# Stick-breaking attention: the scores of two units in one run with both masks behind them, running sums grouped by matrix over both heads

## The chip, the cores and the metric

The kernel runs on one core of one Trainium2 chip. The metric is device time in microseconds; the time before is the median of 3 runs. A profile of one execution gives busy times, waits and the order of instructions.

## The reference

The whole program is two transformer blocks over 512 positions of 1024 features, in float32. The first has an MLP, a mixer of windowed attention and gated linear attention, and a second MLP. The second is a stack of two layers; each has a mixer, a cross-attention into 256 memory tokens and a gated MLP with a short convolution. The mixer of the last layer is the one that is changed here: strictly causal stick-breaking attention, 16 heads of 64 features.

```
z = (q . k) * scale                      # per head, 512 x 512
log_beta = log_sigmoid(z)
log_1m   = where(strict, log_sigmoid(-z), 0)
tail     = reverse cumsum(log_1m) - log_1m
a        = where(strict, exp(log_beta + tail), 0)
out      = a @ v
```

In the kernel's terms this is a = exp(z - (softplus(z) of this key and of all later keys up to the query)), with masked places at -1e30 before the exponential.

## The kernel before

**Work of a pair.** Heads are taken in pairs (t = 0 to 7; j = 0, 1 in a pair), since two heads of 64 features fill 128 partitions. The scores lie transposed in PSUM: 128 keys of a block kb down the partitions, the queries kb*128 to 511 along the columns. The four key blocks are dealt to three *units*: unit 0 holds blocks 3 and 2 (128 + 256 columns per head), unit 1 block 1 (384), unit 2 block 0 (512). A unit has two PSUM banks, one per head, which serve for z and then, with the sums added onto them, for the exponent.

**Steps of a unit.**
1. TensorE, `stick_scores(t, u)`: keys times queries in float32 with 64 rows of contraction (L1267; each is recorded as two matmuls, and the two heads use different halves of the array), then one matmul per head with an identity that adds the mask onto the diagonal block (L1272). The last one raises `z_done`. For t > 0 the function first waits for `a_made` of the pair before, that is until ScalarE has read the unit's banks.
2. ScalarE, `soft`: exponential (L1862) and logarithm of 1 + it (L1864), which is softplus.
3. VectorE, `softplus`: a clamp that reads z from PSUM (L2766), then the split of the value in a rounded part `hi` (L2768) and a rest `lo` (L2770). That raises `softplus_cut`.
4. TensorE, `stick_exponent(t, u)`: after waiting for `softplus_cut` it adds the negated sums onto z. L1282 multiplies the unit's own hi and lo by matrix 0 of `od_later` (minus a triangle of ones: sums within the key block), L1291 multiplies the parts of later key blocks by matrix 1 (minus all ones). It raises `arg_ready`.
5. ScalarE, `weights`: exponential into `od_a` (L1868), which raises `a_made`.
6. TensorE, `stick_out(t)`: `od_a` times the values (L1303, 16 matmuls), once all three units of the pair are there; VectorE copies the result out (L2775).

**Order.** Each engine runs its own queue in program order. TensorE's order for a pair is: scores of unit 1, scores of unit 2, `stick_out` of the pair before, exponents of units 0 and 1, scores of unit 0 of the next pair, exponent of unit 2. ScalarE's is soft 1, soft 2, weights 0, weights 1, soft 0 of the next pair, weights 2. VectorE's is softplus 1, softplus 2, copy of the pair before, softplus 0 of the next pair. Ahead of the loop stand the scores of units 0 and 1 of pair 0 and one slab of the value projection (L623 to L625); ScalarE's `soft(0, 1)` is behind a wait for the end of that slab. Behind the loop stands the output projection (L605 to L607), as everywhere else in the program a stream of 512-column matmuls over weight slabs.

Of the kernel before, what the change touches and what calls it, by code (L numbers as in the profile page):

```python
# [15 lines left out]
P = 128  # L16
SEQ = 512
# [8 lines left out]
NB = SEQ // P  # L26
# [36 lines left out]
UNITS = [(3, 2), (1,), (0,)]  # L63
UNIT_COLUMNS = [FAR, 3 * P, 4 * P]
# [36 lines left out]
def block_at(kb):  # L101

    return [2, 1, 0, 0][kb], P if kb == 2 else 0
# [49 lines left out]
def build(nc, wstream, gains, conv_w, lam_in, base, rope, later, gla_masks, alibi, gate_up,  # L153
          x_in, p_in, mem_in, out):
    ctx = ExitStack()
    with ctx:
        def sb(name, shape, dt=FP32, scope=ctx):
            return scope.enter_context(nc.sbuf_tensor(name, shape, dt))

        def sem(name):  # L160
            return ctx.enter_context(nc.semaphore(name))
# [46 lines left out]
        with ExitStack() as s:  # L208
            od_q = sb("od_q", [P, KT, SEQ], FP32, s)
            od_k = sb("od_k", [P, KT, SEQ], FP32, s)  # L210
# [24 lines left out]
        ident_r = sb("ident_r", [P, P], FP32R)  # L235
# [51 lines left out]
        with ExitStack() as s:  # L287
            od_v = sb("od_v", [P, NB, D], FP32, s)
            od_mask = sb("od_mask", [P, 3, P], FP32, s)
            od_later = sb("od_later", [P, 3, P], FP32R, s)  # L290
            od_a = sb("od_a", [P, 2, TRI], FP32, s)
        ps = ctx.enter_context(nc.psum_tensor("ps", [P, 8, SEQ], FP32))
# [93 lines left out]
        z_done = sem("z_done")  # L386
# [4 lines left out]
        a_made = sem("a_made")  # L391
# [14 lines left out]
        def pair_of(c):  # L406

            if AT_MIX1 + MIX1_FIRST <= c < AT_MIX1 + MIX1_FIRST + 2:
                return 0
            if AT_MIX1 + MIX1_SLABS <= c < AT_MIX1 + MIX1_SLABS + DOWN:  # L410
                return [5, 0, 2, 5][c - AT_MIX1 - MIX1_SLABS]
            if AT_EVEN + EVEN_FIRST <= c < AT_EVEN + EVEN_SLABS:
                return 2
            if c == AT_EVEN + EVEN_SLABS:
                return 6
            return 2 * (c % 2)
# [27 lines left out]
        def gl_turned(t, n):  # L444

            return gl_k[:, t, n]
# [33 lines left out]
        def k_to_end():  # L480

            return m1_c[:, 0:2 * SEQ].rearrange("p (t n) -> p t n", t=2)
# [16 lines left out]
        def unit_bank(u):  # L499

            return [4, 6, pair_of(AT_ODD + ODD_SLABS - 2)][u]
# [9 lines left out]
        def unit_parts(t, u):  # L511

            at, w = UNIT_AT[u], UNIT_COLUMNS[u]
            if u == 0 and t % 2 == 0:
                tiles = (od_s_even, od_hi_even, od_lo_even)
            else:
                tiles = (od_s, od_hi, od_lo)
            return [tile[:, :, at:at + w] for tile in tiles]
# [5 lines left out]
        def spread(ap, n):  # L524

            return ap.unsqueeze(1).to_broadcast([ap.shape[0], n, ap.shape[1]])
# [53 lines left out]
        def _(pe):  # L580
            n = {"cut": 0, "cuts": 0, "op": 0, "h": 0, "sq": 0, "job": 0, "it": 0, "xsq": 0, "norm": 0, "pair": 0}
            mm_ = nc.tensor.matmul
# [31 lines left out]
            def to_positions(c, cols=256, beside={}):  # L614

                start_slab(c)
                wh = w_hi[:, c % 4, :].rearrange("p (k n) -> p k n", k=KT)
                wl = w_lo[:, c % 4, :].rearrange("p (k n) -> p k n", k=KT)
                for r in range(NB):
                    o = acc_rows(c)[:, r, 0:cols]  # L620
                    for k in range(KT):
                        xh, xl = op_hi[:, k, r * P:(r + 1) * P], op_lo[:, k, r * P:(r + 1) * P]
                        mm_(o, xh, wh[:, k, 0:cols], start=(k == 0), stop=False)  # L623
                        mm_(o, xl, wh[:, k, 0:cols], start=False, stop=False)  # L624
                        mm = mm_(o, xh, wl[:, k, 0:cols], start=False, stop=(k == KT - 1))  # L625
                    if r == NB - 1:
                        mm.then_inc(slab_done, 1)
                    if r in beside:
                        beside[r]()
# [307 lines left out]
            for t in range(2):  # L937
                for b in range(NB - 1):
                    mm = nc.tensor.transpose(ps[:, 4 + t, b * P:(b + 1) * P], k_to_end()[:, t, b * P:(b + 1) * P], ident)
# [3 lines left out]
            for b in range(NB - 1):  # L943
                for t in range(2):
                    for j in range(2):
                        h = 2 * t + j
                        mm = mm_(ps[64 * j:64 * j + 64, 6 + t, b * P:(b + 1) * P],
                                 gl_turned(t, slice(b * P + 64 * j, b * P + 64 * j + 64)),
                                 m1_gv[:, b, h * P:(h + 1) * P],
                                 start=True, stop=True)  # L950
# [7 lines left out]
            for b in range(1, NB):  # L958
                for t in range(2):
                    for j in range(2):  # L960
# [3 lines left out]
                            skip_group_check=True)  # L964
            for bp in range(2):
                pe.wait_ge(gl_c_ready, 2 * (LEVELS - MASKED) + bp + 1)
                for j in range(2):
                    for b in range(2):
                        for t in range(2):
                            h, blk = 2 * t + j, 2 * bp + b  # L970
                            mm = mm_(ps[:, h, blk * P:(blk + 1) * P], m1_gv[:, blk, h * P:(h + 1) * P],
                                     gl_a[:, bp, 4 * j + 2 * b + t, :], start=False, stop=(blk == NB - 1),
                                     skip_group_check=True)
# [282 lines left out]
            for d in range(8, 11):  # L1256
                to_positions(AT_ODD + d)

            def stick_scores(t, u):


                if t:
                    pe.wait_ge(a_made, 3 * (t - 1) + u + 1)
                for kb in UNITS[u]:
                    b, at = unit_bank(u), block_at(kb)[1]
                    for j in range(2):
                        mm_(ps[:, b + j, at:at + SEQ - kb * P], od_k[64 * j:64 * j + 64, t, kb * P:(kb + 1) * P],  # L1267
                            od_q[64 * j:64 * j + 64, t, kb * P:SEQ], start=(kb == UNITS[u][0]), stop=False,
                            skip_group_check=True)
                w = len(UNITS[u]) * P  # L1270
                for j in range(2):
                    mm = mm_(ps[:, b + j, 0:w], ident_r[:], spread(od_later[:, 2, :], len(UNITS[u])), start=False,  # L1272
                             stop=True, skip_group_check=True)
                mm.then_inc(z_done, 1)

            def stick_exponent(t, u):

                pe.wait_ge(softplus_cut, 3 * t + u + 1)
                for j in range(2):
                    _, hi, lo = unit_parts(t, u)  # L1280
                    for part in (hi, lo):
                        mm_(ps[:, unit_bank(u) + j, 0:UNIT_COLUMNS[u]], od_later[:, 0, :], part[:, j, :],  # L1282
                            start=False, stop=True, skip_group_check=True)
                    for kb in UNITS[u]:
                        z = block_at(kb)[1]
                        for b in range(kb + 1, NB):
                            (of, at), w = block_at(b), SEQ - b * P
                            a0 = z + (b - kb) * P
                            _, hi, lo = unit_parts(t, of)
                            for part in (hi, lo):  # L1290
                                mm = mm_(ps[:, unit_bank(u) + j, a0:a0 + w], od_later[:, 1, :],  # L1291
                                         part[:, j, at:at + w], start=False, stop=True, skip_group_check=True)
                mm.then_inc(arg_ready, 1)

            def stick_out(t):
                if t >= 2:
                    pe.wait_ge(o_read, t - 1)
                for kb in reversed(range(NB)):
                    (of, at), w = block_at(kb), SEQ - kb * P
                    pe.wait_ge(a_made, 3 * t + of + 1)  # L1300
                    at += UNIT_AT[of]
                    for j in range(2):
                        mm = mm_(ps[64 * j:64 * j + 64, stick_bank(t), kb * P:SEQ],  # L1303
                                 od_v[:, kb, (2 * t + j) * 64:(2 * t + j + 1) * 64], od_a[:, j, at:at + w],
                                 start=(kb == NB - 1), stop=(kb == 0), skip_group_check=True)
                mm.then_inc(stick_ready, 1)

            pe.wait_ge(later_ready, 1)
            stick_scores(0, 0)
            stick_scores(0, 1)  # L1310
            to_positions(AT_ODD + ODD_SLABS - 1)
            n["op"] += KT
            pe.wait_ge(acc_free, AT_ODD + ODD_SLABS + 1)
            for t in range(PAIRS):
                if t:
                    stick_scores(t, 1)
                stick_scores(t, 2)
                if t == 1:
                    pe.wait_ge(acc_free, AT_ODD + ODD_SLABS + 2)
                if t:  # L1320
                    stick_out(t - 1)
                stick_exponent(t, 0)
                stick_exponent(t, 1)
                if t < PAIRS - 1:
                    stick_scores(t + 1, 0)
                stick_exponent(t, 2)
            stick_out(PAIRS - 1)
            project(AT_ODD + ODD_SLABS)
# [6 lines left out]
        def _(act):  # L1335
# [522 lines left out]
            def soft(t, u):  # L1858

                buf, _, _ = unit_parts(t, u)  # L1860
                act.wait_ge(z_done, 3 * t + u + 1)
                f_(buf, unit_z(u), ACT.Exp).then_inc(a_step, 1)  # L1862
                done(a_step)
                f_(buf, buf, ACT.Ln, bias=1.0).then_inc(sp_ready, 1)  # L1864
# [1106 lines left out]
```

## Time and profile before

| | |
|---|---|
| median of 3 runs | 2562.7 us (2562.1 to 2562.7) |
| span of the profiled execution | 2561.3 us |
| PE busy | 2541.6 us, 99% |
| DVE (VectorE) busy | 1596.4 us, 62% |
| ACT (ScalarE) busy | 912.6 us, 36% |
| stick-breaking stretch | about 1875 to 1984 us of the span |

The profiled execution's time is known here by its span; the median of the runs is 1.4 us above it. PE is TensorE's matmuls, PEld its weight loads. Matmuls are pipelined: start times are exact, ends are modelled, so the distance from one start to the next says more than a duration. A matmul row such as `64*128 64x384` has 64 rows of contraction and 384 columns.

### The profile page before, as it was taken

The page shows a single profiled execution, that of the slowest core. Times are in us where ns is not written, and L with a number is a line of the kernel's source. Part 1 is how long each engine was busy: PE and PEld are TensorE (multiplying, and loading weights), DVE is VectorE, ACT ScalarE, POOL GpSimd, SP SyncE. Part 2 cuts the span into 40 slices and gives each one's busy share as a digit, 9 for nine tenths or more (in the row PEclk, how much of TensorE's full clock was granted, in tenths as well). Part 3 has the DMA queues.
Part 4 walks back from the last instruction along what each step waited for, and adds up shares of the span by engine and source line. Part 5 has one row for each costly group of instructions (what it writes and reads, how often), then busy time and mean ns, then how long its engine had stood idle before and what let it go on. Part 6 is the DMA issues. An engine that isn't in the chain of part 4 may idle for free.

```text
span 2561.3 us, 31974 instructions
## 1 busy us (share of the span) xinstructions
PE 2541.6 (99%) x12548; PEld 2107.0 (82%) x12548; DVE 1596.4 (62%) x1976; ACT 912.6 (36%) x1184; POOL 10.2 (0%) x24
## 2 busy tenths in 40 slices
PE   8999999999999999999999999999999999999999
PEld 7888888778888888877898888888886888888887
DVE  6444468866444468677765747476357665775755
ACT  5222234543222245344443423233146343432322
POOL 0000001000000000000000000000000000000000
PEclk9999999999999999999999999999999999999999
DMA  5222233112222232212321232323210232232222
GB/s 182 102 83 99 96 110 120 67 50 96 103 89 98 99 115 101 99 50 99 132 94 63 104 103 82 115 83 123 94 66 13 87 116 83 84 115 83 101 96 82
DMA packets 37410, 241.91 MB, mean 94 GB/s; under 512 B 4416, under 2 KB 7280, under 8 KB 9136
## 3 DMA queue, kind: packets, MB, share of 16 engines
q1 hardware_dynamic: 34736, 233.78, 26.3%
q10 hardware_dynamic: 1920, 5.22, 0.6%
q0 software_dynamic: 640, 1.31, 0.2%
q8 instruction: 81, 1.33, 0.2%
q14 instruction: 33, 0.27, 0.0%
HBM read 236.89 MB, written 2.10 MB: 93 GB/s over the span
## 4 chain that ended last, share of the span: by engine, by line
PE 93%; DVE 5%; ACT 1%; issue 1%; DMA 0%; POOL 0%; DVEq 0%; ACTq 0%
PE ps L605 24%; PE ps L607 24%; PE ps L606 24%; PE ps L1234 1%; PE ps L623 1%; PE ps L625 1%; PE ps L624 1%; PE ps L766 1%; PE ps L1267 1%; PE ps L1291 1%; PE ps L1282 1%; DVE w_lo L2048 1%; PE ps L768 1%; PE ps L767 1%; PE ps L1303 1%
## 5 line engine op out<-in xcount | busy, mean ns | idle before, releaser
L605 PE MATMUL ps<-op_hi,w_hi 128*128 128x512 f32 x2056 | 800.9, 390 | 0.2 <-DVE op_lo L1929 0.2
L606 PE MATMUL ps<-op_lo,w_hi 128*128 128x512 f32 x2056 | 800.5, 389 | 0.0
L607 PE MATMUL ps<-op_hi,w_lo 128*128 128x512 f32 x2056 | 800.4, 389 | 0.0
L1350 ACT ACTIVATE w_hi<-w_raw 128x2048 fp32r<-128x2048 f32 x217 | 414.4, 1911 | 485.2 <-PE ps L607 315.3
L2048 DVE TENSOR_TENSOR w_lo<-w_raw,w_hi 128x2048 fp32r<-128x2048 f32 x217 | 497.0, 2292 | 38.7 <-ACT w_hi L1350 22.3
L605 PEld LDWEIGHTS ps<-op_hi,w_hi 128*128 128x128 f32 x2056 | 386.3, 188 | 81.4 <-issue 1.4
L607 PEld LDWEIGHTS ps<-op_hi,w_lo 128*128 128x128 f32 x2056 | 386.2, 188 | 80.6
L606 PEld LDWEIGHTS ps<-op_lo,w_hi 128*128 128x128 f32 x2056 | 386.3, 188 | 80.3
L2013 DVE SCALAR_TENSOR_TENSOR x<-ps,x 128x512 f32<-128x512 f32 x134 | 92.7, 691 | 310.8 <-PE ps L607 293.0
L605 PE MATMUL ps<-h_hi,w_hi 128*128 128x512 f32 x692 | 269.5, 389 | 0.0
L606 PE MATMUL ps<-h_lo,w_hi 128*128 128x512 f32 x692 | 269.2, 389 | 0.0
L607 PE MATMUL ps<-h_hi,w_lo 128*128 128x512 f32 x692 | 269.2, 389 | 0.0
L2096 DVE TENSOR_TENSOR sil<-ps,rs_x 128x512 f32<-128x512 f32 x44 | 30.4, 692 | 212.2 <-PE ps L607 209.1
L1463 ACT ACTIVATE conv_buf<-u_buf,cw 128x512 f32<-128x512 f32 x88 | 63.2, 726 | 260.9 <-DVE u_buf L2079 260.9
L605 PEld LDWEIGHTS ps<-h_hi,w_hi 128*128 128x128 f32 x692 | 129.9, 188 | 27.6 <-DVE h_lo L2107 0.6
L606 PEld LDWEIGHTS ps<-h_lo,w_hi 128*128 128x128 f32 x692 | 129.9, 188 | 27.0
L607 PEld LDWEIGHTS ps<-h_hi,w_lo 128*128 128x128 f32 x692 | 129.9, 188 | 26.9
L1468 ACT ACTIVATE sil<-sil 128x512 f32<-128x512 f32 x44 | 27.9, 634 | 338.2 <-DVE sil L2096 338.1
L2079 DVE TENSOR_TENSOR u_buf<-ps,rs_x 128x512 f32<-128x512 f32 x44 | 30.4, 692 | 82.1 <-PE ps L607 82.1
L2088 DVE SCALAR_TENSOR_TENSOR conv_buf<-u_buf,cw,conv_buf 128x511 f32<-128x511 f32 x88 | 66.1, 751 | 20.5 <-ACT conv_buf L1463 11.0
L1395 ACT ACTIVATE sq<-x 128x512 f32<-128x512 f32 x80 | 48.3, 623 | 77.8 <-DVE sums L1941 74.1
L2091 DVE SCALAR_TENSOR_TENSOR conv_buf<-u_buf,cw,conv_buf 128x510 f32<-128x510 f32 x88 | 66.0, 750 | 10.5 <-DVE conv_buf L2088 1.4
(373 smaller groups left out, 3085.7 us busy)
## 6 DMA issues: line engine op xcount, KB each, us to landing
w_raw<-in_wstream_dram SPq DMA_DIRECT2D x217, 1024.0 KB, 4.8
cr_m<-in_mem_dram ACTq DMA_DIRECT2D x2, 1024.0 KB, 4.9
w_raw<-in_wstream_dram SPq DMA_DIRECT2D x7, 256.0 KB, 8.0
x<-in_x_dram SPq DMA_DIRECT2D x3, 512.0 KB, 7.3
out_dram<-x SPq DMA_DIRECT2D x3, 512.0 KB, 2.6
m_s<-m_q POOLq DMA_DIRECT2D x16, 64.0 KB, 2.5
ev_s<-in_alibi_dram ACTq DMA_DIRECT2D x1, 1024.0 KB, 4.9
m_c<-in_rope_dram ACTq DMA_DIRECT2D x1, 640.0 KB, 3.9
```

The costliest lines, as they stand in the source:

```text
L605: mm_(o, w_hi[:, c % 4, w], hi[:, k, 0:cols], start=(k == 0), stop=False)
L606: mm_(o, w_hi[:, c % 4, w], lo[:, k, 0:cols], start=False, stop=False)
L607: mm = mm_(o, w_lo[:, c % 4, w], hi[:, k, 0:cols], start=False, stop=(k == kt - 1))
L1350: f_(w_hi[:, c % 4, :], w_raw[:, c % 2, :], ACT.Copy).then_inc(w_hi_ready, 1)
L1395: f_(to[:, n["xsq"] % 2, 0:src.shape[1]], src, ACT.Square).then_inc(xsq_ready, 1)
L1463: f_(conv_buf[:, j, :], u_buf[:, j, :], ACT.Copy, scale=tap).then_inc(tap_ready, 1)
L2013: ins = v.scalar_tensor_tensor(x[:, 2 * d + j, :], acc(c, j), half, x[:, 2 * d + j, :], ALU.mult, ALU.add)
L2048: v.tensor_tensor(w_lo[:, c % 4, :], w_raw[:, c % 2, :], w_hi[:, c % 4, :].bitcast(FP32), ALU.subtract).then_inc(w_ready, 1)
L2079: v.tensor_tensor(u_buf[:, 0, :], acc(c, 0), rs_x[:], ALU.mult).then_inc(scaled_ready, 1)
L2088: v.scalar_tensor_tensor(buf[:, 1:SEQ], u[:, 0:SEQ - 1], w1, buf[:, 1:SEQ], ALU.mult, ALU.add).then_inc(v_step, 1)
L2091: v.scalar_tensor_tensor(buf[:, 2:SEQ], u[:, 0:SEQ - 2], w0, buf[:, 2:SEQ], ALU.mult, ALU.add).then_inc(v_step if j else conv_ready, 1)
L2096: v.tensor_tensor(sil[:, c % 2, :], acc(c, 0), rs_x[:], ALU.mult).then_inc(scaled_ready, 1)
```

## The change

`stick_scores` takes a list of units: it issues the scores of all of them and then the masks of all of them, raising `z_done` after each unit's mask. The wait for `a_made` of each unit stands before that unit's scores, and so ahead of both masks. Units 1 and 2 of a pair (and units 0 and 1 of pair 0) are issued that way. In `stick_exponent` the loops over heads and matrices are exchanged: units 0 and 2 issue all matmuls with matrix 0 for both heads and then all with matrix 1; unit 1 the other way round. Number and sizes of matmuls are the same. ScalarE's and VectorE's programs are not touched.

```diff
-            def stick_scores(t, u):
-                if t:
-                    pe.wait_ge(a_made, 3 * (t - 1) + u + 1)
-                for kb in UNITS[u]:
-                    b, at = unit_bank(u), block_at(kb)[1]
+            def stick_scores(t, units):
+                for u in units:
+                    if t:
+                        pe.wait_ge(a_made, 3 * (t - 1) + u + 1)
+                    for kb in UNITS[u]:
+                        b, at = unit_bank(u), block_at(kb)[1]
+                        for j in range(2):
+                            mm_(ps[:, b + j, at:at + SEQ - kb * P], od_k[64 * j:64 * j + 64, t, kb * P:(kb + 1) * P],
+                                od_q[64 * j:64 * j + 64, t, kb * P:SEQ], start=(kb == UNITS[u][0]), stop=False,
+                                skip_group_check=True)
+                for u in units:
+                    w = len(UNITS[u]) * P
                     for j in range(2):
-                        mm_(ps[:, b + j, at:at + SEQ - kb * P], od_k[64 * j:64 * j + 64, t, kb * P:(kb + 1) * P],
-                            od_q[64 * j:64 * j + 64, t, kb * P:SEQ], start=(kb == UNITS[u][0]), stop=False,
-                            skip_group_check=True)
-                w = len(UNITS[u]) * P
+                        mm = mm_(ps[:, unit_bank(u) + j, 0:w], ident_r[:], spread(od_later[:, 2, :], len(UNITS[u])),
+                                 start=False, stop=True, skip_group_check=True)
+                    mm.then_inc(z_done, 1)
+
+            def sums_within(t, u):
+                _, hi, lo = unit_parts(t, u)
                 for j in range(2):
-                    mm = mm_(ps[:, b + j, 0:w], ident_r[:], spread(od_later[:, 2, :], len(UNITS[u])), start=False,
-                             stop=True, skip_group_check=True)
-                mm.then_inc(z_done, 1)
+                    for part in (hi, lo):
+                        mm = mm_(ps[:, unit_bank(u) + j, 0:UNIT_COLUMNS[u]], od_later[:, 0, :], part[:, j, :],
+                                 start=False, stop=True, skip_group_check=True)
+                return mm
+
+            def sums_of_later(t, u):
+                pairs = [(kb, b) for kb in UNITS[u] for b in range(NB - 1, kb, -1)]
+                for kb, b in pairs:
+                    (of, at), w = block_at(b), SEQ - b * P
+                    a0 = block_at(kb)[1] + (b - kb) * P
+                    _, hi, lo = unit_parts(t, of)
+                    for j in range(2):
+                        for part in (hi, lo):
+                            mm = mm_(ps[:, unit_bank(u) + j, a0:a0 + w], od_later[:, 1, :], part[:, j, at:at + w],
+                                     start=False, stop=True, skip_group_check=True)
+                return mm
 
             def stick_exponent(t, u):
                 pe.wait_ge(softplus_cut, 3 * t + u + 1)
-                for j in range(2):
-                    _, hi, lo = unit_parts(t, u)
-                    for part in (hi, lo):
-                        mm_(ps[:, unit_bank(u) + j, 0:UNIT_COLUMNS[u]], od_later[:, 0, :], part[:, j, :],
-                            start=False, stop=True, skip_group_check=True)
-                    for kb in UNITS[u]:
-                        z = block_at(kb)[1]
-                        for b in range(kb + 1, NB):
-                            (of, at), w = block_at(b), SEQ - b * P
-                            a0 = z + (b - kb) * P
-                            _, hi, lo = unit_parts(t, of)
-                            for part in (hi, lo):
-                                mm = mm_(ps[:, unit_bank(u) + j, a0:a0 + w], od_later[:, 1, :],
-                                         part[:, j, at:at + w], start=False, stop=True, skip_group_check=True)
+                if u == 1:
+                    sums_of_later(t, u)
+                    mm = sums_within(t, u)
+                else:
+                    sums_within(t, u)
+                    mm = sums_of_later(t, u)
                 mm.then_inc(arg_ready, 1)
@@
-            stick_scores(0, 0)
-            stick_scores(0, 1)
+            stick_scores(0, [0, 1])
             to_positions(AT_ODD + ODD_SLABS - 1)
@@
             for t in range(PAIRS):
-                if t:
-                    stick_scores(t, 1)
-                stick_scores(t, 2)
+                stick_scores(t, [1, 2] if t else [2])
@@
                 if t < PAIRS - 1:
-                    stick_scores(t + 1, 0)
+                    stick_scores(t + 1, [0])
                 stick_exponent(t, 2)
```

## Rows read from the trace of the kernel before

**Rows 1.** The page: span, and busy time of TensorE with its instructions.

```profile
span 2561.3 us, 31974 instructions
...
PE 2541.6 (99%) x12548; PEld 2107.0 (82%) x12548; DVE 1596.4 (62%) x1976; ACT 912.6 (36%) x1184; POOL 10.2 (0%) x24
```

**Rows 2.** Timeline: start us, us, instruction; scores of units 1 and 2, pair 2.

```profile
1911.39 0.27 PE L1291 MATMUL ps<-od_lo,od_later 128*128 128x128 f32 x1
1911.59 0.92 PE L1267 MATMUL ps<-od_q,od_k 64*128 64x384 f32 x4
1911.70 1.02 ACT L1868 ACTIVATE od_a<-ps 128x1024 f32<-128x1024 f32 x1 [0.81 <-PE ps L1291]
1912.43 0.44 PE L1272 MATMUL ps<-od_later,ident_r 128*128 128x128 f32 x2
1912.81 1.13 PE L1267 MATMUL ps<-od_q,od_k 64*128 64x512 f32 x4
1912.91 0.81 ACT L1862 ACTIVATE od_s<-ps 128x768 f32<-128x768 f32 x1 [0.19 <-PE ps L1272]
1913.86 0.44 PE L1272 MATMUL ps<-od_later,ident_r 128*128 128x128 f32 x2
...
1914.23 2.37 PE L1303 MATMUL ps<-od_a,od_v 128*64 128x128 f32 x16
```

**Rows 3.** Timeline of the same pair, from VectorE's split of unit 1 on.

```profile
1916.29 0.96 DVE L2770 TENSOR_TENSOR od_lo<-od_s,od_hi 128x768 fp32r<-128x768 f32 x1
...
1917.74 0.39 PE L1282 MATMUL ps<-od_hi,od_later 128*128 128x384 f32 x1
...
1919.27 1.23 DVE L2770 TENSOR_TENSOR od_lo<-od_s,od_hi 128x1024 fp32r<-128x1024 f32 x1
...
1920.55 0.19 PEld L1282 LDWEIGHTS ps<-od_hi,od_later 128*128 128x128 f32 x1
...
1923.23 0.92 PE L1267 MATMUL ps<-od_q,od_k 64*128 64x384 f32 x4
```

**Rows 4.** Timeline of the last pair, t = 7.

```profile
1971.13 0.81 ACT L1862 ACTIVATE od_s<-ps 128x768 f32<-128x768 f32 x1 [0.19 <-PE ps L1272]
...
1977.48 1.23 DVE L2770 TENSOR_TENSOR od_lo<-od_s,od_hi 128x1024 fp32r<-128x1024 f32 x1
...
1978.76 0.19 PEld L1282 LDWEIGHTS ps<-od_hi,od_later 128*128 128x128 f32 x1 [1.17 <-DVE od_lo L2770]
...
1979.10 0.39 PE L1282 MATMUL ps<-od_lo,od_later 128*128 128x512 f32 x1
...
1979.98 0.27 PE L1291 MATMUL ps<-od_lo,od_later 128*128 128x128 f32 x1
...
1980.09 0.45 PE L1282 MATMUL ps<-od_hi,od_later 128*128 128x512 f32 x1
...
1980.38 0.39 PE L1282 MATMUL ps<-od_lo,od_later 128*128 128x512 f32 x1
...
1980.61 0.34 PE L1291 MATMUL ps<-od_hi,od_later 128*128 128x384 f32 x1
...
1981.46 2.37 PE L1303 MATMUL ps<-od_a,od_v 128*64 128x128 f32 x16
```

**Rows 5.** Waits, 1888 to 1984 us: who <- whom: us in total, times, longest.

```profile
ACT od_s L1862 <- PE ps L625: 10.5, 1, 10.5
...
PEld ps L1282 <- DVE od_lo L2770: 3.5, 3, 2.0
```

**Rows 6.** Timeline: scores and mask of unit 0 ahead of the loop.

```profile
1876.30 0.50 PE L1272 MATMUL ps<-od_later,ident_r 128*128 128x256 f32 x2
...
1876.74 0.92 PE L1267 MATMUL ps<-od_q,od_k 64*128 64x384 f32 x4
```

**Rows 7.** Busy time by stretch: length, engines (instructions), granted clock PEclk, DMA.

```profile
1888.00:1900.00 12.00, 10.03 (x68) 8.14 (x66) 7.84 (x9) 6.80 (x8) 0.00 (x0) 1.00 0.00 0
```

## The prediction

> **What bounds the kernel now.** I read the page first, then the stretch of the trace where the changed lines run, then its instructions in order of time. The page gives PE 2541.6 us busy in a span of 2561.3 us [rows 1]. Read alone, that says that a shorter TensorE program is a shorter kernel. But matmul ends are modelled, so a PE that has just been released can still look busy. The question is what releases it inside the stick-breaking stretch, from about 1875 to 1984 us.
>
> Take one pair t of the loop, from the start S of `stick_scores(t, 1)` at 1911.59 to the next one at 1923.23: 11.64 us [rows 2, 3]. Follow it from S. The scores of unit 1 and its mask raise `z_done`, and ScalarE starts its exponential at 1912.91, 1.32 us after S [rows 2]. The two activations and then VectorE's six instructions for units 1 and 2 follow. The last one starts at 1919.27 and ends 1.23 us later, at 1920.50 [rows 3]. PE loads the weights of `stick_exponent(t, 2)` at 1920.55, 0.05 us after that end. From there to the next S are 2.68 us. So 1.32 + 7.64 + 2.68 = 11.64 us: the whole period is one loop through PE, ScalarE and VectorE.
>
> Is this loop the bound, or does it only keep step with a PE that is full? The last pair answers. There no scores stand between `stick_exponent(7, 1)` and `stick_exponent(7, 2)`, and PE visibly waits, 1.17 us, for `od_lo`. From the start of unit 1's exponential (1971.13) to that release (1978.76) are 7.63 us, the lag of VectorE's end (1977.48 + 1.23 = 1978.71) to the weight load is again 0.05 us, and from the load to the instruction after the exponent matmuls (1981.46) are 2.70 us [rows 4]. The undisturbed pair has the same three numbers. Hence its slack is about zero: what delays `z_done` of unit 1 lengthens every pair by the same amount, and PE time saved ahead of `stick_exponent(t, 2)` buys nothing. The view of waits hides this: it books only 3 such waits on VectorE, 3.5 us in all [rows 5].
>
> **The change part by part.** No matmul is added or removed; 8 pairs run.
>
> *Where PE waits for the previous weights.* `stick_scores(t, 2)` waits for `a_made` of (t-1, 2), ScalarE's exponential over 1024 columns. It started at 1911.70, 0.11 us after S, took 1.02 us, and the scores of unit 2 started at 1912.81, 0.09 us after its end [rows 2]. Before, unit 1's mask ran in this time, and `z_done` of unit 1 was out before the wait. After, that mask stands behind the wait and behind the scores of unit 2. This is the largest term.
>
> *Delay of `z_done` of unit 1.* After the change the exponential starts about 0.06 us behind S (see the running sums), takes 1.02, and the release takes 0.09: scores of unit 2 start at S + 1.17. From their start to a mask matmul are 1.05 us (1912.81 to 1913.86), and from the mask's start to ScalarE's exponential 0.48 us (1912.43 to 1912.91) [rows 2]. Sum: 1.17 + 1.05 + 0.48 = 2.70 us where it was 1.32: +1.38. Bounds: without the wait for `a_made` only the scores of unit 2 would stand in between, 512 columns in the four passes that the rows show (128 more columns cost 1912.81 to 1913.86 less 1911.59 to 1912.43 = 0.21 us, so 512 cost 0.85): +0.85. If restarting after the wait costs what it costs the exponent matmuls, 0.34 from first to second instead of 0.23 [rows 4]: +1.49. I take +1.38, the wait being in the code and its end in the rows.
>
> *Fewer switches among scores and masks.* Going from a 64-row score matmul to the mask and back has a price: the mask of unit 1 holds PE from 1912.43 to 1912.81, 0.38 us, where its 256 columns stream in 0.11 (at one pass, 512 take 0.21). That is 0.27 too much, and a group of scores has a fill of its own: 1911.59 to 1912.43 is 0.84 us for 384 columns in four passes, 0.64, so 0.20 [rows 2]. The Trainium skill, "TensorEngine Tiling (Array Packing)", Key Properties, says that a change of tiling mode drains the engine. The trace agrees (0.38 us for 0.11); by that rule alone the change would save one round of it per pair, about 0.45 us, and some 3.6 us in all. In the loop the room that this frees is filled by the wait for `a_made`, so for t >= 1 I take zero. Once, before the loop, it is real: `stick_scores(0, [0, 1])` stands behind TensorE's own projection. There the mask of unit 0 took 1876.30 to 1876.74, 0.44 us for 0.21 of streaming [rows 6], plus the second fill of 0.20: -0.43 us. It counts because ScalarE's `soft(0, 1)` waits 10.5 us for the end of the following projection [rows 5].
>
> *Running sums by matrix.* Before, `stick_exponent(t, 2)` goes from 128-column sums of the second matrix back to 512-column ones of the first between the heads. The steps are 0.11 (1979.98 to 1980.09) and 0.29 (to 1980.38), then 0.23 (to 1980.61) [rows 4]. With 0.055 (a quarter of the streaming of 512) and 0.23 as the regular steps for 128 and 512 columns, the return costs 0.11 us. After the change I add starts: 0.34 + 3 x 0.23 for the four 512-column ones, 4 x 0.055, 4 x 0.115, 4 x 0.17 for later sums of 128, 256, 384, and 0.145 for the switch to scores (1911.39 to 1911.59 less 0.055 [rows 2]). That is 2.54 us for 2.68: -0.14. Bounds: 0 (another such return appears where widths grow from 128 to 256) and -0.29 (every overhead but one restart and one switch gone: 5120 columns in 2.13 us, + 0.11 + 0.145). The last matmul is now 384 wide and ends 0.34 + 0.03 us after its start, while S comes 0.16 + 0.145 after it: the exponential starts 0.06 us after S, used above. The same grouping in units 0 and 1 saves about 0.11 us each, on PE time that waits anyway: zero. If that cover were gone it would be 0.22 x 8 = 1.8 us gained.
>
> *Is something else late next?* `stick_exponent(t, 1)` waits for VectorE's unit 1: 1916.29 + 0.96 is 4.34 us after ScalarE's start [rows 3], so 2.70 + 4.34 + 0.05 = 7.09 us after S. From its start to the load of `stick_exponent(t, 2)` it took 1917.74 to 1920.55, 2.81 us with `stick_scores(t + 1, 0)` in it; with 0.11 for the restart that ends at 10.01. VectorE releases at 2.70 + 7.64 = 10.34. So PE waits twice per pair, VectorE stays the releaser, with 0.33 us to spare. Behind the waiting PE stand `stick_out(t - 1)` (2.37 us, [rows 2]) and `stick_exponent(t, 0)`; their customers, ScalarE's weights 0 and VectorE's copy, have over 1 us of room.
>
> *Sum.* Period after: 2.70 + 7.64 + 2.54 = 12.88 us, +1.24. Seven pairs carry it (t = 1 to 7): +8.7. Pair 0 has unit 1 long done and only gets the shorter exponent: -0.14. Start: -0.43. Total +8.1 us, span 2569.4. Behind the stretch PE streams weights as before, so it is passed on whole. The span shown is 1.4 us under the median; added to the median of 2562.7, the time is 2570.8 us.
>
> **The rivals.**
> 1. *The loop has slack, PE is the bound.* Then the added delay is absorbed, and the grouping pays: 8 x 0.36 + 0.43 = -3.3 us, 2559.4, not slower. It decides only if the slack per pair is over 1.2 us; for it speaks PE's 99% [rows 1], against it the equal 0.05 us and 2.7 us in a pair that waits and in one that seems not to [rows 3, 4]. Slack s under that takes off 7s. Chance 5%.
> 2. *`a_made` holds nothing back.* Scores 2 follow scores 1 directly, +0.85 instead of +1.38: 7 x (0.85 - 0.14) - 0.57 = +4.4 us, 2567.1, within the resolution. For it: the scores of unit 2 may have started at 1912.81 because the mask took that long. Against: the exponential ended at 1912.72, and it can't start before the last exponent matmul [rows 2]. With a large gain from grouping this is also the low edge. Chance 9%.
> 3. *Two restarts make PE late again.* If restarts cost over 0.33 us more than counted in `stick_exponent(t, 1)`, or the wait for `a_made` costs a restart of its own, each 0.1 us is 0.7 us: +9 to +12, 2572 to 2575. Chance 11%.
> 4. *The clock falls.* PE now stands for about 1 us and twice 0.3 us per pair. In 1888 to 1900 us, with waits for VectorE of that size, the granted clock was 1.00, the 2.4 GHz level [rows 7]. At the 1.2 GHz level the roughly 9 us of streaming in a pair (a period of 11.64 less waits and fills) would double: 7 x 9 = some +60 us, 2630. The Trainium skill, "TensorE: Matmul & The Clock Gate", in "Why this matters for your kernels", warns of idle gaps between bursts of matmuls; no row here shows a fall. Chance 1%.
>
> **How the numbers follow.** The forecast has 74%; its own range, from +1.38 (-0.06, +0.11) and -0.14 (+0.14, -0.15) times 7, less 0.57, is +6.6 to +9.9: 2569.3 to 2572.6. The 80% range adds part of rivals 2 and 3: 2567.5 to 2573.5. A measurement of this kernel tells about 0.2%, 5.1 us, from no change. Slower by more: forecast, 3 and 4, 86%, less 1 for a mixture with rival 2: 85%. Within: rival 2, most of rival 1: 13%. Faster by more: 2%, rival 1 with rival 2.
>
> **What the profile after would show.** Right: period from S to S near 12.9 us; ScalarE's exponential of unit 1 starting 2.6 to 2.8 us after S; the first score matmul of unit 2 within 0.1 us of the end of ScalarE's weights; the view of waits full of PE on `od_lo`, seven or more at unit 1 (about 1 us) and at unit 2 (about 0.3 us); 7.6 us from that exponential to the load of `stick_exponent(t, 2)`; 2.5 us from there to S; the projection before the loop 0.4 us earlier. Wrong: a period under 11.6 us (rival 1); scores of unit 2 in one run with unit 1 (rival 2); PE reaching `stick_exponent(t, 2)` behind VectorE (rival 3); a granted clock under 1 (rival 4).

## The result, and the profile after

The changed kernel takes 2572.4 us (median of 5 runs, 2571.38 to 2575.3) against 2562.7 us (5 runs, 2561.55 to 2562.85): 9.7 us more. The ratio of the runs is 1.0041, 95% interval 1.0029 to 1.0054: slower (the quotient of the two medians is 1.0038). The forecast was 2570.8 us, with a range of 2567.5 to 2573.5.

The page of the kernel after, its span and its busy time by engine:

```profile
span 2570.6 us, 31974 instructions
...
PE 2543.8 (99%) x12548; PEld 2105.2 (82%) x12548; DVE 1596.4 (62%) x1976; ACT 912.0 (35%) x1184; POOL 10.2 (0%) x24
```

Beside [rows 1] nothing seems to have happened: the same instructions, the same 99% on PE, 2 us more of it, and a span 9.3 us longer. Busy shares of the whole run don't tell this story. Over the stick-breaking stretch alone PE's share does fall, from 93.0 of 96 us (1888 to 1984) to 95.2 of 105 us (1888 to 1993), but only the order in time says why. The timeline of the kernel after, the same pair as in [rows 2, 3] (start us, us, engine, line, operation). L1267 are still the scores; the masks are now L1273, the sums within a block L1282, the later ones L1295, ScalarE's activations L1874, L1876 and L1880, VectorE's split L2782:

```profile
1912.14 0.92 PE L1267 MATMUL ps<-od_q,od_k 64*128 64x384 f32 x4
1912.25 1.02 ACT L1880 ACTIVATE od_a<-ps 128x1024 f32<-128x1024 f32 x1 [1.22 <-PE ps L1295]
...
1913.33 1.13 PE L1267 MATMUL ps<-od_q,od_k 64*128 64x512 f32 x4 [0.27 <-ACT od_a L1880]
...
1914.39 0.66 PE L1273 MATMUL ps<-od_later,ident_r 128*128 128x128 f32 x4
1914.86 0.81 ACT L1874 ACTIVATE od_s<-ps 128x768 f32<-128x768 f32 x1 [1.59 <-PE ps L1273]
...
1918.24 0.96 DVE L2782 TENSOR_TENSOR od_lo<-od_s,od_hi 128x768 fp32r<-128x768 f32 x1
...
1919.25 0.19 PEld L1295 LDWEIGHTS ps<-od_hi_even,od_later 128*128 128x128 f32 x1 [0.75 <-DVE od_lo L2782]
...
1921.21 1.23 DVE L2782 TENSOR_TENSOR od_lo<-od_s,od_hi 128x1024 fp32r<-128x1024 f32 x1
...
1922.49 0.19 PEld L1282 LDWEIGHTS ps<-od_hi,od_later 128*128 128x128 f32 x1 [0.28 <-DVE od_lo L2782]
...
1925.24 0.92 PE L1267 MATMUL ps<-od_q,od_k 64*128 64x384 f32 x4
```

The reader is to see four things. The period from S to S is 25.24 - 12.14 = 13.10 us; it was 11.64. ScalarE's weights of the pair before end at 13.27, and the scores of unit 2 follow at 13.33, with PE released by them. Unit 1's exponential starts 2.72 us after S; it was 1.32. And from there to the weight load of unit 2's exponent are 22.49 - 14.86 = 7.63 us, what they were. PE's weight loads now stand waiting for VectorE's split twice in the pair, for 0.75 and 0.28 us, where the same pair before shows no such wait.

The view of waits of the kernel after, over the stretch (who <- whom: us in total, times, longest):

```profile
PEld ps L1295 <- DVE od_lo L2782: 7.2, 8, 2.0
...
PEld ps L1267 <- ACT od_a L1880: 6.2, 7, 0.9
...
PEld ps L1282 <- DVE od_lo L2782: 3.6, 8, 1.7
```

Seven of the eight pairs wait for ScalarE's weights (`od_a`). All eight wait for VectorE at unit 1 (L1295) and at unit 2 (L1282); [rows 5] had three waits for VectorE in all.

Where the span's 9.3 us lie: seven pairs at 1.45 each are 10.15 us more, pair 0 about 0.05 more; 0.4 less from the run of units 0 and 1 ahead of the loop; and 0.5 less that was there before any changed instruction ran (the first score matmul starts at 1874.91, before at 1875.45), which belongs to the execution and not to the change.

### The profile page after: what moved, and what is told of

Its sections match the earlier page's. It is cut to its first block, busy times and chain, and to the rows that moved or that the text cites. A ratio compares the mean times of both kernels' runs of the same rounds, so it can differ in the third digit from the quotient of the medians.

```text
span 2570.6 us, 31974 instructions
## 1 busy us (share of the span) xinstructions
PE 2543.8 (99%) x12548; PEld 2105.2 (82%) x12548; DVE 1596.4 (62%) x1976; ACT 912.0 (35%) x1184; POOL 10.2 (0%) x24
## 4 chain that ended last, share of the span: by engine, by line
PE 90%; DVE 6%; ACT 2%; issue 1%; DMA 0%; DVEq 0%; ACTq 0%
PE ps L605 24%; PE ps L606 24%; PE ps L607 24%; PE ps L1234 1%; PE ps L623 1%; PE ps L625 1%; PE ps L624 1%; PE ps L766 1%; DVE w_lo L2060 1%; PE ps L768 1%; PE ps L767 1%; DVE od_lo L2782 1%; DVE od_s L2778 1%; PE ps L816 1%; PE ps L1195 1%
```

## The experiments

Each kernel was timed 5 to 11 times beside the kernel before on the same chip; differences are of medians, while a ratio with its 95% interval comes from all the runs and is not the quotient of the medians. The first four kernels shared a chip (before: 2562.24 us there), and so did the last three (2562.11 us).

**1. The run of scores alone.** `stick_scores` and its calls from the change, `stick_exponent` from before.

```diff
 # stick_scores(t, units), stick_scores(0, [0, 1]), stick_scores(t, [1, 2] if t else [2]): as in the change
-                if u == 1:
-                    sums_of_later(t, u)
-                    mm = sums_within(t, u)
...
+                for j in range(2):
+                    for part in (hi, lo):
+                        ...                        # L1282, then L1291, head by head
```

> Half of the change alone: units 1 and 2 (0 and 1 ahead of the loop) in one run with both masks behind it; exponent matmuls in the order of the kernel before. Zero slack in the loop through PE, ScalarE and VectorE: the wait for a_made ahead of both masks delays unit 1's exponential from 1.32 to about 2.75 us after S; period 11.64 + 1.4 = 13.05 us, 7 pairs +10, start -0.4: +9 to +10 us, as much as the whole change. Rival (PE is the bound): the run saves a switch per pair, -0.4 us in the loop, time same or a little less than before.

2571.16 us, +8.9; ratio 1.0038 (1.0024 to 1.0052). Its timeline (here ScalarE's exponential is L1860, its weights L1866):

```profile
1911.07 0.92 PE L1267 MATMUL ps<-od_q,od_k 64*128 64x384 f32 x4
...
1912.26 1.13 PE L1267 MATMUL ps<-od_q,od_k 64*128 64x512 f32 x4 [0.27 <-ACT od_a L1866]
...
1913.79 0.81 ACT L1860 ACTIVATE od_s<-ps 128x768 f32<-128x768 f32 x1 [1.59 <-PE ps L1273]
...
1924.11 0.92 PE L1267 MATMUL ps<-od_q,od_k 64*128 64x384 f32 x4
```

Period 13.04 us, the exponential 2.72 us after S, as expected; the time is just short of the +9 to +10 us. This half is nearly the whole of the loss.

**2. The grouped sums alone.** The change's `stick_exponent`, `sums_within` and `sums_of_later`; scores and masks as before.

```diff
 # stick_scores(t, u) and its calls: as before
+                if u == 1:
+                    sums_of_later(t, u)
+                    mm = sums_within(t, u)
+                else:
+                    sums_within(t, u)
+                    mm = sums_of_later(t, u)
```

> The other half alone: scores and masks as before, exponent matmuls grouped by matrix over both heads. If going back to the first matrix costs 0.11 us, as the prediction had it, the exponent of unit 2 shortens to 2.54 us and the time falls by 8 x 0.14 = 1.1 us. If the cost belongs to 128-column matmuls in a row (each asks for a weight load of its own, 0.11 us apart), four in a row cost what two pairs of them did: exponent of unit 2 2.7 to 2.75 us, period 11.64 to 11.75, time +0 to +0.6 us.

2562.9 us, +0.7; ratio 1.0004 (0.9995 to 1.0013). By time alone this decides little, by the trace more (sums within a block L1281):

```profile
1910.96 0.92 PE L1267 MATMUL ps<-od_q,od_k 64*128 64x384 f32 x4
...
1919.94 0.19 PEld L1281 LDWEIGHTS ps<-od_hi,od_later 128*128 128x128 f32 x1
...
1922.69 0.92 PE L1267 MATMUL ps<-od_q,od_k 64*128 64x384 f32 x4
```

The period is 11.73 us, and from the load of the exponent of unit 2 to S are 2.75 us, the figures of the second expectation. The grouping saves nothing there; it costs 0.07 us. The return to the first matrix, which the prediction priced, isn't what costs.

**3. VectorE's rounding of unit 1 twice.** Kernel before, 0.6 us more in the chain and nothing on PE.

```diff
-                v.tensor_copy(hi, buf).then_inc(v_step, 1)
-                done(v_step)
+                for _ in range(2 if u == 1 else 1):
+                    v.tensor_copy(hi, buf).then_inc(v_step, 1)
+                    done(v_step)
```

> The kernel before with VectorE's rounding of unit 1 done twice in every pair: 0.56 us of VectorE work and its 0.04 us of waiting in the chain, nothing on PE. Zero slack: period 11.64 + 0.6 = 12.24 us, 8 pairs: +4.8 us. PE is the bound and the chain has slack (rival 1 of the prediction, over 1.2 us): period 11.64, no change.

2567.06 us, +4.8; ratio 1.0020 (1.0011 to 1.0029). Its timeline:

```profile
1911.93 0.92 PE L1267 MATMUL ps<-od_q,od_k 64*128 64x384 f32 x4
...
1916.03 1.16 DVE L2769 CAST od_hi<-od_s 128x768 fp32r<-128x768 f32 x2
...
1921.48 0.19 PEld L1282 LDWEIGHTS ps<-od_hi,od_later 128*128 128x128 f32 x1 [0.31 <-DVE od_lo L2771]
...
1924.16 0.92 PE L1267 MATMUL ps<-od_q,od_k 64*128 64x384 f32 x4
```

In the kernel before the rounding of unit 1 is one instruction:

```profile
1915.69 0.56 DVE L2768 CAST od_hi<-od_s 128x768 fp32r<-128x768 f32 x1
```

Two take 1.16 us, 0.60 more, and the period is 12.23 us, 0.59 more. An engine that is busy 62% of the span was given 0.6 us more per pair, and all of it came out at the end: the chain has no slack that the trace can tell, although PE's row says 99%.

**4. Exponent matmuls ordered by width.** Kernel before; a 128-column matmul never follows another while a wider one is left, so the matrix alternates.

```diff
+                wide = [...]        # (bank, first column, width, matrix, moving part) of all matmuls of the unit
+                short = [m for m in wide if m[2] == P]
+                rest = [m for m in wide if m[2] > P]
+                order = []
+                for m in rest:
+                    order.append(m)
+                    if short:
+                        order.append(short.pop(0))
+                order += short
```

> Scores and masks as before; exponent matmuls ordered so that a 128-column one never follows another where a wider one is left, which changes the matrix at almost every matmul. If changing the matrix costs: exponent of unit 2 gets longer, by up to 0.1 us a change, time up. If 128-column matmuls in a row cost (weight loads 0.11 us apart against 0.055 us of streaming): the exponent of unit 2 falls from 2.68 to about 2.5 us, period about 11.45 to 11.5, time -1.2 to -1.5 us.

2562.89 us, +0.6; ratio 1.0004 (0.9995 to 1.0013). Both expectations missed. Nothing is gained: from the load of the exponent of unit 2 (1919.70) to S (1922.48) are 2.78 us, where 2.5 were expected. And the many changes of matrix don't cost up to 0.1 us each either. The steps tell what does cost; they follow below, under the third point.

**5. The wait for `a_made` alone, earlier.** Kernel before, no work moved.

```diff
                 w = len(UNITS[u]) * P
+                if t and u == 1:
+                    pe.wait_ge(a_made, 3 * (t - 1) + 3)
                 for j in range(2):
                     mm = mm_(ps[:, b + j, 0:w], ident_r[:], ...
```

> The kernel before with one wait moved: PE waits for a_made of the pair before (unit 2) already ahead of unit 1's mask, so scores 1, wait, mask 1, scores 2, mask 2. No work and no order of matmuls changes. Zero slack and the wait open at about S + 1.22: mask 1 at 1.22 instead of 0.84, unit 1's exponential at S + 1.70 instead of 1.32, period 12.02 us, 7 pairs: +2.7 us. Rival (the wait was open in any case when PE came to it): no change.

2564.47 us, +2.4; ratio 1.0009 (1.0000 to 1.0018), a difference at the edge of what the runs can tell, so the trace has to carry it. Its timeline (mask L1274, ScalarE's weights L1870, exponential L1864):

```profile
1922.66 0.92 PE L1267 MATMUL ps<-od_q,od_k 64*128 64x384 f32 x4
1922.77 1.02 ACT L1870 ACTIVATE od_a<-ps 128x1024 f32<-128x1024 f32 x1 [0.80 <-PE ps L1293]
...
1923.85 0.44 PE L1274 MATMUL ps<-od_later,ident_r 128*128 128x128 f32 x2 [0.27 <-ACT od_a L1870]
...
1924.32 0.81 ACT L1864 ACTIVATE od_s<-ps 128x768 f32<-128x768 f32 x1 [0.53 <-PE ps L1274]
...
1934.64 0.92 PE L1267 MATMUL ps<-od_q,od_k 64*128 64x384 f32 x4
```

The mask starts 0.06 us after the weights end, the exponential 1.66 us after S, and the period is 11.98 us, in every pair. The shift of the exponential and the growth of the period are both 0.34 us: one line that issues no work costs what it shifts `z_done` by.

**6. Unit 1's scores before the exponent of unit 2.** Unit 1 got buffers of its own for odd pairs, in free memory, so that ScalarE doesn't overwrite parts that PE still reads, and ScalarE's order was changed to match.

```diff
 # in the loop of TensorE, pair t
-                if t:
-                    stick_scores(t, 1)
                 stick_scores(t, 2)
...
                 if t < PAIRS - 1:
                     stick_scores(t + 1, 0)
+                    stick_scores(t + 1, 1)
                 stick_exponent(t, 2)
 # not shown: the buffers, and ScalarE's order (soft(t + 1, 1) ahead of weights(t, 2))
```

> The kernel before with unit 1's scores of the next pair moved ahead of the exponent of unit 2 (own buffers for unit 1 in odd pairs, ScalarE's order changed to match). VectorE's chain for unit 1 now starts some 4 us earlier, so it can't be late. What stays is PE's own wait for the weights of unit 2 with nothing in front of it: exponent of unit 2 to scores of unit 2 3.9 us from start to start, and the other steps of a pair 9.0 us: period about 12.9 us, +9 us. If only VectorE's chain counted and the wait were harmless: period 11.64 or less, time same or lower.

2570.13 us, +8.0; ratio 1.0032 (1.0019 to 1.0044). In its timeline (scores L1273, weights L1873, `stick_out` L1309) PE stands between the exponent of unit 2 and the scores of unit 2:

```profile
1927.33 1.02 ACT L1873 ACTIVATE od_a<-ps 128x1024 f32<-128x1024 f32 x1 [0.48 <-PE ps L1297]
...
1928.41 1.13 PE L1273 MATMUL ps<-od_q,od_k 64*128 64x512 f32 x4 [1.11 <-ACT od_a L1873]
...
1929.84 2.37 PE L1309 MATMUL ps<-od_a,od_v 128*64 128x128 f32 x16
```

S to S (of unit 1's scores) is 1923.47 to 1936.34, 12.87 us. VectorE's chain for unit 1 is early now, and yet the pair is nearly as long as in the change (13.10 us): PE waits 1.11 us for the weights with nothing to do. Unit 1's scores are what fills that wait in the kernel before.

**7. Mask first.** Scores of units 1 and 2 in a run, as in the change, but unit 1's mask ahead of its scores, so that `z_done` of unit 1 leaves with its last score matmul.

```diff
+                    if u == 1:
+                        for j in range(2):
+                            mm_(ps[:, unit_bank(u) + j, 0:w], ident_r[:], spread(...), start=True, stop=False, ...)
                     for kb in UNITS[u]:
                         ...                                     # scores; start=False for unit 1
+                    if u == 1:
+                        mm.then_inc(z_done, 1)
```

> Scores of units 1 and 2 without a mask between them, as in the change, but unit 1's mask is issued ahead of its scores and z_done of unit 1 leaves with its last score matmul, before the wait for a_made. Exponents as before. If the cost of the change is the late z_done of unit 1 and not the run itself: unit 1's exponential at about S + 1.1 to 1.3 us, period 11.5 to 11.7 us, time -1 to +0.5 us. If the run of two units costs by itself: +9 us as the change.

2561.63 us, -0.5; ratio 0.9999 (0.9990 to 1.0008). Its timeline (mask first L1267, scores L1272, mask of unit 2 L1279, exponential L1866, ScalarE's weights L1872, split L2774, exponent L1289):

```profile
1921.72 0.39 PE L1267 MATMUL ps<-od_later,ident_r 128*128 128x128 f32 x2
...
1921.92 1.02 ACT L1872 ACTIVATE od_a<-ps 128x1024 f32<-128x1024 f32 x1 [0.80 <-PE ps L1298]
1922.04 2.09 PE L1272 MATMUL ps<-od_q,od_k 64*128 64x384 f32 x8
...
1923.00 0.30 PEld L1272 LDWEIGHTS ps<-od_q,od_k 64*128 64x128 f32 x4 [0.66 <-ACT od_a L1872]
1923.00 0.81 ACT L1866 ACTIVATE od_s<-ps 128x768 f32<-128x768 f32 x1
...
1929.35 1.23 DVE L2774 TENSOR_TENSOR od_lo<-od_s,od_hi 128x1024 fp32r<-128x1024 f32 x1
...
1930.73 0.19 PEld L1289 LDWEIGHTS ps<-od_hi,od_later 128*128 128x128 f32 x1
...
1933.65 2.09 PE L1272 MATMUL ps<-od_q,od_k 64*128 64x384 f32 x8
```

The run of two units costs nothing by itself. The period is 11.61 us, and here PE loads the weights 0.15 us after VectorE's end (1930.58), not 0.05: the chain through VectorE is 0.1 us ahead and no longer the bound. PE isn't simply full either. The load for unit 2's scores stands until ScalarE's weights are done (1922.94) and comes at 1923.00, and these scores start 0.96 us after those of unit 1, of which some 0.3 us are waiting (an estimate: 384 columns take 0.64 us in the prediction's sum). What is left is a second loop, through PE and ScalarE's weights: weights 1.02 us, hand-over 0.06, scores of unit 2 to the load of its exponent 7.73 (1923.00 to 1930.73), and from there 2.80 to the start of the next weights (1933.53). Together they are 11.61 us.

The kernel before runs this second loop too. Its four parts there are 1.02, 0.09, 7.74 and 2.79 us, 11.64 in all, where the 0.09 [rows 2] is 0.03 more than the hand-over needs. So the kernel before has two loops of nearly the same length, 11.64 us through VectorE and 11.61 through the weights of unit 2.

## Why the prediction was right, point by point

**The loop without slack** was right. It rested on two lags, 0.05 us and 2.7 us, that were equal in a pair that waits and in one that seems not to. Experiment 3 shows it directly: +0.60 us of work in the chain, +0.59 in the period, +4.8 us in time. The equal lags alone were thinner evidence than they looked, because PE would have arrived at that load within some 0.03 us of the same moment on its own (the second loop of experiment 7). Rival 1 is refuted: by its account experiment 3 would have changed nothing. Experiment 7 adds a limit that the prediction didn't see: with the chain through VectorE 0.1 us ahead, the loop through ScalarE's weights holds the period at 11.61 us.

**The wait for `a_made`** was right in place and size: scores of unit 2 at S + 1.19 (forecast 1.17), unit 1's exponential at S + 2.72 (2.70). Rival 2 had them follow at once; in experiment 5 the wait alone, moved ahead of the mask, costs 2.4 us, and in experiment 6, with nothing in front of it, PE stands 1.11 us. In the change both parts of the delay are there: 1.19 instead of 0.84 us until PE may go on, and then the 1.06 us of unit 2's scores ahead of the mask. The two halves add up: the period grew by 1.40 us in experiment 1 and by 0.09 in experiment 2, by 1.46 in the change; in time +8.9 and +0.7 (the latter not clear of zero) beside +9.7.

**The running sums** are the step that failed. I put -0.14 us for the exponent of unit 2; it measured +0.07 (2.75 us from load to S, before 2.68). Eight pairs times 0.21 us are 1.7 us, about the 1.6 by which 2570.8 fell short; the rest of the sum held. The mistake was to charge 0.11 us to the return to the first matrix. The timeline of the kernel after, from that exponent:

```profile
1923.30 0.40 PE L1282 MATMUL ps<-od_lo,od_later 128*128 128x512 f32 x1
...
1923.54 0.22 PE L1295 MATMUL ps<-od_hi_even,od_later 128*128 128x128 f32 x1
1923.54 0.19 PEld L1295 LDWEIGHTS ps<-od_lo_even,od_later 128*128 128x128 f32 x1
1923.60 0.27 PE L1295 MATMUL ps<-od_lo_even,od_later 128*128 128x128 f32 x1
1923.65 0.19 PEld L1295 LDWEIGHTS ps<-od_hi_even,od_later 128*128 128x128 f32 x1
1923.71 0.28 PE L1295 MATMUL ps<-od_hi_even,od_later 128*128 128x128 f32 x1
1923.76 0.19 PEld L1295 LDWEIGHTS ps<-od_lo_even,od_later 128*128 128x128 f32 x1
1923.82 0.28 PE L1295 MATMUL ps<-od_lo_even,od_later 128*128 128x128 f32 x1
...
1923.93 0.33 PE L1295 MATMUL ps<-od_hi_even,od_later 128*128 128x256 f32 x1
...
1924.10 0.28 PE L1295 MATMUL ps<-od_lo_even,od_later 128*128 128x256 f32 x1
...
1924.97 0.33 PE L1295 MATMUL ps<-od_lo,od_later 128*128 128x384 f32 x1
```

There is no return to the first matrix here, and the steps of 128 columns are 0.06, then 0.11, 0.11, 0.11, and the first one of 256 columns 0.17 instead of 0.11. And in experiment 4, where the matrix alternates:

```profile
1919.82 0.39 PE L1301 MATMUL ps<-od_hi,od_later 128*128 128x512 f32 x1
...
1920.05 0.22 PE L1301 MATMUL ps<-od_hi_even,od_later 128*128 128x128 f32 x1
...
1920.11 0.45 PE L1301 MATMUL ps<-od_lo,od_later 128*128 128x512 f32 x1
...
1920.39 0.22 PE L1301 MATMUL ps<-od_lo_even,od_later 128*128 128x128 f32 x1
```

The second 512-column matmul, right behind a 128-column one, takes 0.28 us where 0.23 is the rule. Each 128-column matmul takes some 0.06 us more than its 0.055 of streaming, be it alone between wide ones (its 0.06 us, and 0.05 more on the next step), in a pair (before: 0.11 more for two) or in a run of four (0.22 for four). That fits weight loads that can't follow each other closer than the 0.11 us of these rows (1923.54, 1923.65, 1923.76), and every matmul has one. The Trainium skill, "TensorE: Matmul & The Clock Gate", section "LDWEIGHTS (loading the stationary operand)", gives the weight load as its number of columns divided by 1.2 GHz; for 128 columns that is an estimate of 107 ns. The spacing of the loads in the trace, 0.11 us, agrees with it, while the record of one load is 0.19 us long. None of the three orders saves this. What was measured is the spacing in three orders; that weight loads are its cause is argued, not isolated.

So the 0.14 us weren't saved, and 0.07 us came on top at the end of the exponent. Before, a narrow matmul stands last, and its step with the switch to the scores is 0.20 us (1911.39 to 1911.59, [rows 2]); in the change a 384-column one stands last, with 0.27 (1924.97 to 1925.24).

**The run ahead of the loop** was right in sign and size: from the first score matmul to the projection 2.01 us instead of 2.41, -0.40 for a forecast of -0.43.

**Next in line** (rival 3) was right to be left at a small chance: PE was ready 0.28 us before VectorE at unit 2 (forecast 0.33). At unit 1 it waited 0.75 us, not about 1. **The clock** stayed at 1.00 in the profile after (rival 4).

## What to carry to other kernels

An engine at 99% can still be held by a loop through two engines at 62% and 36%. Before counting what matmuls you save, compare the lags at the hand-over in an iteration that visibly waits with one that doesn't. The surer test is to lengthen the other engine's part a little and see whether the period follows (experiment 3). When instructions are grouped to save switches, ask what each of them releases and which wait it is moved behind; here a mask of 0.4 us filled a wait, and its signal started the chain that bounds the pair. If a group is wanted, put into it only work that nobody is waiting for, or let the signal leave first (experiment 7).

## What the runs showed that was not expected

The two loops of the kernel before lie 0.03 us apart (11.64 and 11.61 us), so shortening the one through VectorE alone gains next to nothing, as experiment 7 did; no kernel tried here beats it by more than the measurement can tell. A 128-column matmul with its own weight load cost about 0.11 us in all three orders tried, while one of 256 columns behind another such took 0.11 to 0.13, near the 0.11 that it streams.
